# Three edits to a fused three-block network kernel: a weight tile split one stage earlier, residual rows scaled between convolved tiles, and the last norm done by token halves

## The chip, the cores and the metric

The kernel runs on one core of one Trainium2 chip. The metric is the time of one execution in device microseconds (us). TensorE is PE (its weight loads PEld), VectorE DVE, ScalarE ACT, GpSimd POOL; SyncE (SP) issues most DMAs.

## What is computed

Three different residual blocks run one after the other over 1024 tokens of width 1024, all in float32. Each block normalises, projects in, mixes, projects out, and adds a feed-forward part; then comes that block's own final norm. Cut to what the change touches:

```python
def second_block(x, w_in, ln1_g, ln2_g, lnf_g, ...):
    h = rmsnorm_2(x, ln1_g[l])
    p = h @ w_in[l]                       # 32 tiles of 128 columns
    ...                                   # qk = silu(causal conv of 4 taps), recurrences
    x = x + y @ w_out[l]
    h = rmsnorm_2(x, ln2_g[l])
    x = x + (jax.nn.silu(h @ w_gate[l]) * (h @ w_up[l])) @ w_down[l]
    return rmsnorm_2(x, lnf_g)

def third_block(x, ...):
    h = rms_norm(x, norm_mix[l])
    proj = jnp.einsum("bsd,dc->bsc", h, w_in[l])   # 25 tiles
    ...
    ff = jnp.square(jax.nn.relu(jnp.einsum("bsd,df->bsf", h, w_ff1[l])))
    x = x + jnp.einsum("bsf,fd->bsd", ff, w_ff2[l])
    return rms_norm(x, norm_final)
```

## The kernel before

**Layout and stages.** Activations lie transposed: the residual `g.h` is 8 tiles of 128 features (partitions) by 1024 tokens. The program is a row of stages; a stage ends when all five engines meet at a barrier. The stages that matter are the dense in-projections (`dense`, called as in1, in2, in3) and the second half of each block (`back`, as ff1, ff2, ff3: out-projection, middle norm, feed-forward part). `tidy` at the very end, and `sweep` inside a stage, clear the semaphores that the stage before used, half of them on POOL and half on SP.

**A product.** float32 products run as three fp32r matmuls, so every 128x1024 weight tile is split into a rounded part and a rest: `split_hi` (ACT, L186) and then `split_lo` (POOL, L192), into one of two weight buffers. `product` (L221 to L223) makes 48 matmuls of 128x512 for one output tile, 24 for each half of the tokens, into one of two groups of four PSUM banks. A tile needs three things: its split weights (`lo`), a free accumulator (`free`, given when DVE has read the tile before it in the same banks), and its right-hand side.

**From ff1 to in2, and from ff2 to in3.** `back` already starts the next dense stage: it loads four weight tiles of the next in-projection, splits two of them and makes their two products (tiles 0 and 1 of the dense stage) on the unnormalised residual; the norm's factor per token is applied when DVE empties the accumulator. Between and behind these products come the sums of squares (matmuls with a matrix of ones, L278) and the roots (`roots_of` on ACT: logarithm and exponential, each with a table load, L291 to L300; `scale_of` on DVE). The dense stage starts with `begun=True`: `grant` on POOL gives the starting counts of the semaphores (L166, L173), tile 2 is then split, and DVE empties tiles 0 and 1. The residual itself must still be multiplied by the norm's factor and gain: `scaled_rows` (L324), 8 instructions of 128x1024 on DVE, whose factor lies in `c.tot[0]`. When all 8 are done (`n_whole`), SP stores the residual (`spill`, at tile 7, L400).

**in2.** Tiles 0 to 3 are convolved (`convolved`): DVE reads the accumulator (L470), runs 4 taps (L479, L481, L482), ACT applies Silu (L418), stores the tile, and only then splits the next weights, since one ACT loop does both. The 8 `scaled_rows` stand behind the L470 of tile 0. From tile 4 on, one DVE instruction a tile is left (L502), and from tile 8 on a side job (`rwkv_beside`) runs beside the products.

**in3.** Tiles 0 to 8 are not convolved (L489), and 2 `scaled_rows` already stand behind each of tiles 0 to 3; a side job (`spatial_beside`, L4242 to L4312) starts at tile 0.

**ff3 and the end.** ff3 has no next stage. Its last tile (48 matmuls) is added to the residual over all tokens (L1243), squared on ACT (L337), added to the sum (L362), summed over the features on PE (L278), and turned into the root on ACT (L291, L294). The stage ends. `last_norm` is a stage of its own: DVE multiplies 6 rows of 128x1024 (L1298), ACT and POOL two (L1304, L1312), SP stores 8 rows of 512 KB (L1319), and the sweeps of ff3's semaphores run in it; `tidy` follows.

## Time and profile before

| | |
|---|---|
| median of 3 runs | 4217.23 us (4214.6 to 4221.69) |
| the profiled execution, its own time | 4217.12 us |
| its span (first to last instruction) | 4215.4 us |
| mean granted PE clock over the span | 0.94 |
| busy: PE, DVE, ACT, POOL | 88%, 65%, 38%, 26% |

A row of the timeline reads: start in us from the beginning of the span, length in us, engine, line, operation, output <- input with its size, and a count where equal ones in a row are merged; in square brackets the engine's idle time before it and what ended that. "SPq", "POOLq" are the engines' instruction queues. In the rows on one source line the durations are ns (least/median/greatest), then the first and last start in us.

### The profile page before, as it was taken

Reading aid. Unit: us, or ns where it says so; the run is one execution under the profiler, and the core shown is the slowest. Engines: PE = TensorE matmul, PEld = TensorE weight load, DVE = VectorE, ACT = ScalarE, POOL = GpSimd, SP = SyncE. Lnnn points to the kernel's source line nnn. Section 1 sums busy time; section 2 is a strip of 40 time slices with the busy share of each in tenths; the row PEclk is TensorE's granted clock in tenths of the full one; section 3 lists DMA queues with packets and bytes.
Section 4 is the critical chain, followed back from the end, with each engine's and each line's share of the span. In section 5 each row is a group of like instructions: output and inputs, shape, how many; then the busy total and the mean of one; then the engine's idle time right before and its main releaser. Section 6 shows DMA issues by size and latency. Waiting matters only on the chain. (4 is left out here: it accounts for less than half of the span.)

```text
span 4215.4 us, 46865 instructions
## 1 busy us (share of the span) xinstructions
PE 3710.3 (88%) x17658; PEld 3087.9 (73%) x17658; DVE 2728.3 (65%) x2977; ACT 1617.3 (38%) x2171; POOL 1113.3 (26%) x875
## 2 busy tenths in 40 slices
PE   9965999999989986856999999999933979999997
PEld 8953778788878776745788877878823957887886
DVE  3668688767544555366678877544859447887673
ACT  2503444433322234235433343354144564444332
POOL 1110222444212210200232244222120412224441
PEclk9987999999999998978999999999966989999998
DMA  4310255644143322242333344222272442556531
GB/s 137 104 51 15 66 160 160 211 154 134 46 140 109 112 83 58 76 152 78 106 101 111 105 156 144 80 85 85 90 185 52 137 149 75 170 160 196 163 120 60
DMA packets 525702, 482.38 MB, mean 114 GB/s; under 512 B 103237, under 2 KB 415045, under 8 KB 525481
## 3 DMA queue, kind: packets, MB, share of 16 engines
q1 hardware_dynamic: 516120, 445.22, 34.6%
q10 hardware_dynamic: 9360, 34.21, 2.0%
q8 instruction: 139, 2.28, 0.2%
q14 instruction: 83, 0.67, 0.1%
HBM read 321.77 MB, written 157.60 MB: 114 GB/s over the span
## 5 line engine op out<-in xcount | busy, mean ns | idle before, releaser
L921 POOL TENSOR_TENSOR c_wlo<-ff_spare,c_whi 128x512 fp32r<-128x512 f32 x200 | 322.0, 1611 | 573.9 <-ACT c_whi L755 573.6
L979 PE MATMUL c_acc<-c_hi,c_whi 128*128 128x512 f32 x928 | 362.4, 391 | 8.8 <-issue 8.8
L981 PE MATMUL c_acc<-c_lo,c_whi 128*128 128x512 f32 x928 | 361.6, 390 | 0.0
L982 PE MATMUL c_acc<-c_hi,c_wlo 128*128 128x512 f32 x928 | 361.5, 390 | 0.0
L192 POOL TENSOR_TENSOR w_wlo<-w_raw,w_whi 128x1024 fp32r<-128x1024 f32 x60 | 156.1, 2601 | 676.5 <-ACT w_whi L186 676.5
L755 ACT ACTIVATE c_whi<-ff_spare 128x512 fp32r<-128x512 f32 x315 | 198.0, 629 | 343.8 <-PE c_acc L982 329.9
L979 PE MATMUL c_acc<-ff_quad,c_whi 128*128 128x512 f32 x696 | 275.7, 396 | 18.4 <-DVE ff_quad L1219 5.5
L1150 DVE TENSOR_TENSOR h<-h,c_acc 128x512 f32<-128x512 f32 x265 | 176.8, 681 | 164.3 <-PE c_acc L982 164.2
L981 PE MATMUL c_acc<-ff_quad,c_whi 128*128 128x512 f32 x696 | 274.0, 394 | 0.0
L982 PE MATMUL c_acc<-ff_quad,c_wlo 128*128 128x512 f32 x696 | 274.0, 394 | 0.0
L192 POOL TENSOR_TENSOR c_wlo<-c_raw,c_whi 128x1024 fp32r<-128x1024 f32 (+1 forms) x53 | 129.4, 2441 | 451.9 <-ACT c_whi L186 451.9
L921 POOL TENSOR_TENSOR w_wlo<-ff_spare,w_whi 128x512 fp32r<-128x512 f32 x99 | 162.8, 1646 | 273.2 <-ACT w_whi L755 273.1
L221 PE MATMUL c_acc<-c_hi,w_whi 128*128 128x512 f32 x512 | 205.9, 402 | 12.3 <-POOL w_wlo L192 12.3
L979 PEld LDWEIGHTS c_acc<-c_hi,c_whi 128*128 128x128 f32 x928 | 174.7, 188 | 48.0 <-issue 11.2
L186 ACT ACTIVATE w_whi<-w_raw 128x1024 fp32r<-128x1024 f32 x60 | 63.5, 1059 | 361.3 <-PE c_acc L223 323.2
L982 PEld LDWEIGHTS c_acc<-c_hi,c_wlo 128*128 128x128 f32 x928 | 174.5, 188 | 36.5
L981 PEld LDWEIGHTS c_acc<-c_lo,c_whi 128*128 128x128 f32 x928 | 174.6, 188 | 35.9
L222 PE MATMUL c_acc<-c_lo,w_whi 128*128 128x512 f32 x512 | 200.6, 392 | 0.0
L223 PE MATMUL c_acc<-c_hi,w_wlo 128*128 128x512 f32 x512 | 200.4, 391 | 0.0
L221 PE MATMUL c_acc<-pair,w_whi 128*128 128x348 f32 (+1 forms) x512 | 177.1, 346 | 20.3 <-POOLq L166 20.3
L979 PE MATMUL c_acc<-c_hi,w_whi 128*128 128x512 f32 x448 | 174.6, 390 | 4.1 <-issue 4.1
L502 DVE TENSOR_TENSOR c_xs<-c_acc,c_xs 128x1024 f32<-128x1024 f32 x33 | 40.4, 1225 | 207.3 <-PE c_acc L223 198.1
(720 smaller groups left out, 10069.5 us busy)
## 6 DMA issues: line engine op xcount, KB each, us to landing
c_xs<-hidden SPq DMA_DIRECT2D x67, 1024.0 KB, 8.5
hidden<-c_xs SPq DMA_DIRECT2D x32, 1024.0 KB, 5.4
hidden<-h SPq DMA_DIRECT2D x62, 512.0 KB, 2.8
proj<-c_xs ACTq DMA_DIRECT2D x49, 512.0 KB, 2.6
w_raw<-in_w_in SPq DMA_DIRECT2D x48, 512.0 KB, 4.2
c_raw<-in_w_ff SPq DMA_DIRECT2D x36, 512.0 KB, 5.3
ff_spare<-in_w_ff SPq DMA_DIRECT2D x28, 512.0 KB, 6.7
h<-proj SPq DMA_DIRECT2D x25, 512.0 KB, 5.9
```

Source lines behind the costliest of these rows:

```text
L186: act.activation(s.whi[b][:, 0:kt, :], raw[:, 0:kt, :], ACT.Copy).then_inc(s.hi[b], 1)
L192: pool.tensor_tensor(s.wlo[b][:, 0:kt, :], raw[:, 0:kt, :], s.whi[b][:, 0:kt, :].bitcast(F32), ALU.subtract).then_inc(s.lo[b], 1)
L221: pe.matmul(out, s.whi[b][:, k, :], x_hi, start=(k == 0), stop=False)
L222: pe.matmul(out, s.whi[b][:, k, :], x_lo, start=False, stop=False)
L223: mm = pe.matmul(out, s.wlo[b][:, k, :], x_hi, start=False, stop=(k == kt - 1))
L502: dve.tensor_tensor(sliced(stg[b][:, 0:T], T), acc(b), sliced(g.inv[:, 0:T], T), ALU.mult)\
L755: act.activation(ring(s.whi, n), weight_of(n), ACT.Copy).then_inc(s["w_up"], 1)
L921: pool.tensor_tensor(ring(s.wlo, n), weight_of(n), ring(s.whi, n).bitcast(F32), ALU.subtract)\
L979: pe.matmul(to, hi[:, k, :], q_hi[q][:, k, :], start=fresh and k == 0, stop=False, skip_group_check=not fresh)
L981: pe.matmul(to, hi[:, k, :], q_lo[q][:, k, :], start=False, stop=False, skip_group_check=not fresh)
L982: mm = pe.matmul(to, lo[:, k, :], q_hi[q][:, k, :], start=False, stop=k == HK - 1, skip_group_check=not fresh)
L1150: tt(h, h, bank(p, name_), ALU.add).then_inc(s["ev"], 1)
```

## The change

1. ff1 and ff2 also split the third weight tile of the next in-projection (`split_hi` and `split_lo` for `total + 1`), ahead of the roots; the dense stage leaves the split of its tile 2 out, and `grant` gives one more count for it.
2. The norm's factor moves from `c.tot[0]` to `c.sq`. In a convolved start (in2) the 8 `scaled_rows` no longer stand behind the first L470: 2 follow behind the taps of each of tiles 0 to 3.
3. `last_norm` is gone. ff3 makes its last tile by halves of 512 tokens: 24 matmuls, then the ones-matmuls of the 7 rows so far, then the other 24. Each half is added, squared, summed, and rooted by itself, the root once into PSUM (for DVE) and once into SBUF (for POOL). DVE multiplies 12 half rows in place, POOL 4, and SP stores 16 pieces of 256 KB. ff3's 86 semaphores (75 before) are now cleared in `tidy`.

```diff
             pool.sem_inc(s.landed[b], 16)
+        pool.sem_inc(s.hi[0], 1)
+        pool.sem_inc(s.lo[0], 1)
...
-    to = c.inv[:, 0:SEQ] if how == "one" else c.tot[0][:, 0:SEQ]
+    to = c.inv[:, 0:SEQ] if how == "one" else c.sq
...
-        dve.scalar_tensor_tensor(h, h, g.par[:, gain + k:gain + k + 1], c.tot[0][:, 0:SEQ], ALU.mult, ALU.mult)\
+        dve.scalar_tensor_tensor(h, h, g.par[:, gain + k:gain + k + 1], c.sq, ALU.mult, ALU.mult)\
            .then_inc(s["n_whole"], 1)
...
-                    if it + 2 < tiles:
+                    if it + 2 < tiles and not (begun and it == 0):
                         split_hi(act, s, it % 2, it // 2 + 1, KD)
...
-                    split_lo(pool, s, it % 2, it // 2, KD)
+                    if not (begun and it == 2):
+                        split_lo(pool, s, it % 2, it // 2, KD)
...
-                    if it == 0 and head is not None:
-                        scaled_rows(dve, s, g, c, head_gain, off)
-                        dve.wait_ge(s["n_whole"], KD)
...
                        .then_inc(s[f"conv{b}"], 1)
+                    if it < 4 and head == "given":
+                        scaled_rows(dve, s, g, c, head_gain, off, (2 * it, 2 * it + 1))
...
+BY_POOL = (2, 5)
+LAST = ("f_made", "f_add", "f_sq", "f_sum", "f_log", "f_root", "f_copy", "f_gain", "f_dve", "f_pool", "f_out")
...
+                if ending is not None:
+                    for j in range(2):
+                        for n, k in enumerate(k for k in range(KD) if k not in BY_POOL):
+                            sp.wait_ge(s["f_dve"], (KD - len(BY_POOL)) * j + n + 1)
+                            sp.dma_start(ending[1][k * P:k * P + P, j * HALF_T:j * HALF_T + HALF_T], part(k, j))\
+                              .then_inc(s["f_out"], 16)
+                            if k - 1 in BY_POOL:
+                                n = BY_POOL.index(k - 1)
+                                sp.wait_ge(s["f_pool"], len(BY_POOL) * j + n + 1)
+                                sp.dma_start(ending[1][(k - 1) * P:k * P, j * HALF_T:j * HALF_T + HALF_T], part(k - 1, j))\
+                                  .then_inc(s["f_out"], 16)
+                    sp.wait_ge(s["f_out"], 16 * 2 * KD)
 
...
+                if ending is not None:
+                    gain = ending[0]
+                    for k in BY_POOL:
+                        act.activation(hk(k), hk(k), ACT.Copy, scale=g.par[:, gain + k:gain + k + 1]).then_inc(s["f_gain"], 1)
+                    act.wait_ge(s["n_eps"], 1)
+                    act.wait_ge(s["n_tot_a"], KD - 2)
+                    for j in range(2):
+                        act.wait_ge(s["f_add"], j + 1)
+                        act.activation(half(c.sq, j), part(KD - 1, j), ACT.Square).then_inc(s["f_sq"], 1)
+                        act.wait_ge(s["f_sum"], j + 1)
+                        act.activation(half(c.inv, j), s.psum[:, 2 + j, :], ACT.Ln, scale=1.0 / D, bias=c.low[:, 0:1])\
+                           .then_inc(s["f_log"], 1)
+                        act.wait_ge(s["f_log"], j + 1)
+                        act.activation(s.psum[:, 2 + j, :], half(c.inv, j), ACT.Exp, scale=-0.5).then_inc(s["f_root"], 1)
+                        act.activation(half(c.inv, j), half(c.inv, j), ACT.Exp, scale=-0.5).then_inc(s["f_copy"], 1)
                 if then is not None:
                     split_hi(act, s, 0, total, KD)
-                tail_scalar(act, s, g, end, KD - 1)
+                    tail_scalar(act, s, g, end, KD - 1)
                 if then is not None:
                     split_hi(act, s, 1, total, KD)
-                roots_of(act, s, c, how)
+                    split_hi(act, s, 0, total + 1, KD)
+                    roots_of(act, s, c, how)
...
+                    split_lo(pool, s, 0, total + 1, KD)
+                if ending is not None:
+                    for j in range(2):
+                        for n, k in enumerate(BY_POOL):
+                            pool.wait_ge(s["f_gain"], n + 1)
+                            pool.wait_ge(s["f_copy"], j + 1)
+                            pool.tensor_tensor(part(k, j), part(k, j), half(c.inv, j), ALU.mult).then_inc(s["f_pool"], 1)
...
+                def last_tile(it):
+                    def part_of(j, k):
+                        w_hi, w_lo, to = s.whi[1][:, k, :], s.wlo[1][:, k, :], s.psum[:, 4 + j, :]
+                        pe.matmul(to, w_hi, half(xhi[k], j), start=k == 0, stop=False)
+                        pe.matmul(to, w_hi, half(xlo[k], j), start=False, stop=False)
+                        return pe.matmul(to, w_lo, half(xhi[k], j), start=False, stop=k == last_k - 1)
+
+                    def squares(j):
+                        pe.wait_ge(s["f_sq"], j + 1)
+                        pe.matmul(s.psum[:, 2 + j, :], g.ones[:, :], half(c.sq, j), start=False, stop=True)\
+                          .then_inc(s["f_sum"], 1)
+
+                    pe.wait_ge(s.lo[1], it + 2)
+                    pe.wait_ge(s.free[1], it + 1)
+                    for k in range(last_k):
+                        mm = part_of(0, k)
+                    mm.then_inc(s["f_made"], 1)
+                    pe.wait_ge(s["n_tot_a"], KD - 2)
+                    for j in range(2):
+                        pe.matmul(s.psum[:, 2 + j, :], g.ones[:, :], half(c.tot[0], j), start=True, stop=False)
+                    for k in range(last_k):
+                        if k == last_k - 2:
+                            squares(0)
+                        mm = part_of(1, k)
+                    mm.then_inc(s["f_made"], 1)
+                    squares(1)
+
...
-                        product(pe, s, b, outs + j, xhi, xlo, T, last_k, each=rest if j == 0 and b == 0 else None)
+                        if ending is None or (j, b) != (KD // 2 - 1, 1):
+                            product(pe, s, b, outs + j, xhi, xlo, T, last_k, each=rest if j == 0 and b == 0 else None)
+                if ending is not None:
+                    last_tile(outs + KD // 2 - 1)
                 if then is not None:
                     product(pe, s, 0, total, *u, T, KD, halves_of="n")
                     pe.wait_ge(s["n_tot_b"], KD - 1)
-                pe.wait_ge(s["n_tot_a"], KD - 1)
-                sums_of(pe, s, g, c, how)
-                if then is not None:
+                    pe.wait_ge(s["n_tot_a"], KD - 1)
+                    sums_of(pe, s, g, c, how)
                     product(pe, s, 1, total, *u, T, KD)
...
+                        if ending is not None and k == KD - 1:
+                            return
...
-def last_norm(nc, g, c, gain, out):
...
+                if ending is not None:
+                    def added(j):
+                        dve.wait_ge(s["f_made"], j + 1)
+                        tt(part(KD - 1, j), part(KD - 1, j), s.psum[:, 4 + j, :], ALU.add).then_inc(s["f_add"], 1)
+
+                    def whole(j):
+                        gain = ending[0]
+                        dve.wait_ge(s["f_root"], j + 1)
+                        for k in range(KD):
+                            if k == KD - 1:
+                                dve.wait_ge(s["f_sq"], j + 1)
+                            if k not in BY_POOL:
+                                stt(part(k, j), part(k, j), g.par[:, gain + k:gain + k + 1], s.psum[:, 2 + j, :], ALU.mult,
+                                    ALU.mult).then_inc(s["f_dve"], 1)
+
+                    added(0)
+                    added(1)
+                    whole(0)
+                    whole(1)
 
 
...
-    back_half(nc, g, a, c, 3, 0, "w_out_3", "w_ff1_3", "w_ff2_3", 4 * KD, False, None, None, dram, early=early, restore=kept)
-    g.use(6, False)
-    last_norm(nc, g, c, g.col["gf3"], out)
+    back_half(nc, g, a, c, 3, 0, "w_out_3", "w_ff1_3", "w_ff2_3", 4 * KD, False, None, None, dram, early=early, restore=kept,
+              ending=(g.col["gf3"], out))
...
```

**Order of instructions, DVE, start of in2** (`c_acc` is the accumulator, `c_xs` holds the convolution's rows, `par` the taps and gains). Before:

```order
L387 MEMSET c_xs 128x1027
L470 TENSOR_TENSOR c_xs<-c_acc,c_xs 128x1024
L324 SCALAR_TENSOR_TENSOR h<-h,par,c_xs 128x1024 x8
L108 ISA
L479 TENSOR_SCALAR c_xs<-c_xs,par 128x1024
L481 SCALAR_TENSOR_TENSOR c_xs<-c_xs,par 128x1024 x2
L482 SCALAR_TENSOR_TENSOR c_xs<-c_xs,par 128x1024
L470 TENSOR_TENSOR c_xs<-c_acc,c_xs 128x1024
```

After the change:

```order
L389 MEMSET c_xs 128x1027
L473 TENSOR_TENSOR c_xs<-c_acc,c_xs 128x1024
L108 ISA
L479 TENSOR_SCALAR c_xs<-c_xs,par 128x1024
L481 SCALAR_TENSOR_TENSOR c_xs<-c_xs,par 128x1024 x2
L482 SCALAR_TENSOR_TENSOR c_xs<-c_xs,par 128x1024
L326 SCALAR_TENSOR_TENSOR h<-h,par,c_xs 128x1024 x2
L473 TENSOR_TENSOR c_xs<-c_acc,c_xs 128x1024
```

The 8 multiplications of `h` have left the place between the first read of the accumulator and the taps; two now stand behind the taps of tile 0, and two behind those of each of the next three.

**Order of instructions, ACT, end of ff1 and start of in2** (`w_whi` is the rounded half of a weight tile). Before:

```order
L186 ACTIVATE w_whi<-w_raw 128x1024
L291 ACT_TABLE_LOAD
L291 ACTIVATE c_xs<-c_acc,c_low 128x1024
L294 ACT_TABLE_LOAD
L294 ACTIVATE c_xs<-c_xs 128x1024
L298 ACT_TABLE_LOAD
L298 ACTIVATE c_xs<-c_xs,c_low 128x1024
L300 ACT_TABLE_LOAD
L300 ACTIVATE c_xs<-c_xs 128x1024
L631 UNCONDITIONAL_BRANCH
L412 UNCONDITIONAL_BRANCH
L186 ACTIVATE w_whi<-w_raw 128x1024
L418 ACT_TABLE_LOAD
L418 ACTIVATE c_xs<-c_xs 128x1024
L422 DMA proj<-c_xs 128x1024
L186 ACTIVATE w_whi<-w_raw 128x1024
```

After the change:

```order
L188 ACTIVATE w_whi<-w_raw 128x1024 x2
L293 ACT_TABLE_LOAD
L293 ACTIVATE c_xs<-c_acc,c_low 128x1024
L296 ACT_TABLE_LOAD
L296 ACTIVATE c_xs<-c_xs 128x1024
L300 ACT_TABLE_LOAD
L300 ACTIVATE c_xs<-c_xs,c_low 128x1024
L302 ACT_TABLE_LOAD
L302 ACTIVATE c_xs<-c_xs 128x1024
L637 UNCONDITIONAL_BRANCH
L414 UNCONDITIONAL_BRANCH
L420 ACT_TABLE_LOAD
L420 ACTIVATE c_xs<-c_xs 128x1024
L424 DMA proj<-c_xs 128x1024
L188 ACTIVATE w_whi<-w_raw 128x1024
```

One weight split has moved from behind the stage's end (the first instruction of in2) to ahead of the first table load of the roots.

**Order of instructions, ACT, end of ff3 and the last norm.** Before:

```order
L337 ACTIVATE c_xs<-h 128x1024 x3
L291 ACT_TABLE_LOAD
L291 ACTIVATE c_xs<-c_acc,c_low 128x1024
L294 ACT_TABLE_LOAD
L294 ACTIVATE c_xs<-c_xs 128x1024
L631 UNCONDITIONAL_BRANCH
L1301 UNCONDITIONAL_BRANCH
L1304 ACTIVATE flat<-h,par 128x1024 x2
```

After the change:

```order
L339 ACTIVATE c_xs<-h 128x1024 x2
L931 ACTIVATE h<-h,par 128x1024 x2
L936 ACTIVATE c_xs<-h 128x512
L938 ACT_TABLE_LOAD
L938 ACTIVATE c_xs<-c_acc,c_low 128x512
L941 ACT_TABLE_LOAD
L941 ACTIVATE c_acc<-c_xs 128x512
```

The same seven rows (from the square to the exponential into `c_xs`) follow once more for the second half; two multiplications by the gain stand ahead of the first square. There are four table loads where there were two.

**The same place, POOL** (L45 and L53 ISA are the clearing of semaphores). Before:

```order
L192 TENSOR_TENSOR c_wlo<-c_raw,c_whi 128x1024 x8
L631 UNCONDITIONAL_BRANCH
L1307 UNCONDITIONAL_BRANCH
L45 ISA x38
L1312 TENSOR_TENSOR flat<-flat,c_xs 128x1024 x2
L1294 UNCONDITIONAL_BRANCH
L50 UNCONDITIONAL_BRANCH
L53 ISA x2
```

After the change:

```order
L955 TENSOR_TENSOR c_wlo<-ff_spare,c_whi 128x512 x9
L194 TENSOR_TENSOR c_wlo<-c_raw,c_whi 128x1024 x8
L978 TENSOR_TENSOR h<-h,c_xs 128x512 x4
L637 UNCONDITIONAL_BRANCH
L50 UNCONDITIONAL_BRANCH
L53 ISA x43
L49 UNCONDITIONAL_BRANCH
```

The 38 clearings ahead of POOL's multiplications are gone, and 43 stand behind the last barrier but one, where 2 stood.

## Rows read from the trace of the kernel before

**Rows 1.** Page, busy time of each engine.
```profile
PE 3710.3 (88%) x17658; PEld 3087.9 (73%) x17658; DVE 2728.3 (65%) x2977; ACT 1617.3 (38%) x2171; POOL 1113.3 (26%) x875
```
**Rows 2.** Busy time by stretch, the start of in2; column before DMA: granted PE clock.
```profile
1175.00:1200.00 25.00, 12.83 (x49) 10.19 (x49) 23.96 (x18) 4.45 (x4) 5.28 (x2) 0.87 0.13 43
```
**Rows 3.** Timeline, PE, the start of in2.
```profile
1179.89 0.79 PE L221 MATMUL c_acc<-c_hi,w_whi 128*128 128x512 f32 x1 [4.99 <-POOL w_wlo L192]
...
1199.92 0.79 PE L221 MATMUL c_acc<-c_hi,w_whi 128*128 128x512 f32 x1 [7.28 <-POOL w_wlo L192]
```
**Rows 4.** Timeline, DVE, the start of in2.
```profile
1176.42 1.22 DVE L470 TENSOR_TENSOR c_xs<-c_acc,c_xs 128x1024 f32<-128x1024 f32 x1
1177.56 11.74 DVE L324 SCALAR_TENSOR_TENSOR h<-h,par,c_xs 128x1024 f32<-128x1024 f32 x8
...
1190.31 2.60 DVE L481 SCALAR_TENSOR_TENSOR c_xs<-c_xs,par 128x1024 f32<-128x1024 f32 x2
...
1196.39 4.57 DVE L481 SCALAR_TENSOR_TENSOR c_xs<-c_xs,par 128x1024 f32<-128x1024 f32 x2
...
1212.93 1.23 DVE L470 TENSOR_TENSOR c_xs<-c_acc,c_xs 128x1024 f32<-128x1024 f32 x1 [2.56 <-PE c_acc L223]
...
1223.81 1.23 DVE L502 TENSOR_TENSOR c_xs<-c_acc,c_xs 128x1024 f32<-128x1024 f32 x1 [2.77 <-PE c_acc L223]
```
**Rows 5.** Timeline, ACT, end of ff1 and start of in2.
```profile
1162.37 1.28 ACT L291 ACT_TABLE_LOAD   x1 [7.28 <-PE c_acc L278]
...
1194.27 1.06 ACT L418 ACTIVATE c_xs<-c_xs 128x1024 f32<-128x1024 f32 x1 [15.54 <-DVE c_xs L482]
...
1195.80 1.06 ACT L186 ACTIVATE w_whi<-w_raw 128x1024 fp32r<-128x1024 f32 x1 [0.47 <-ACT c_xs L418]
```
**Rows 6.** Timeline, POOL, the start of in2.
```profile
1196.93 2.94 POOL L192 TENSOR_TENSOR w_wlo<-w_raw,w_whi 128x1024 fp32r<-128x1024 f32 x1 [17.09 <-ACT w_whi L186]
```
**Rows 7.** Timeline, PE, after pauses of about 3 us (in ff2 and ff3).
```profile
2515.62 0.47 PE L979 MATMUL c_acc<-ff_quad,c_whi 128*128 128x512 f32 x1 [2.77 <-DVE h L1105]
...
3569.12 0.67 PE L979 MATMUL c_acc<-ff_quad,c_whi 128*128 128x512 f32 x1 [3.25 <-issue]
```
**Rows 8.** Loads of in2's third and fourth weight tiles in ff1 (L179), landing.
```profile
L179 SPq DMA_DIRECT2D w_raw<-in_w_in x2: 368/368/368, 1147.1 to 1158.0; - x2
...
DMA to landing us min/median/max: 4.0/4.1/4.1
```
**Rows 9.** Store of the whole residual (L400, twice in the program), landing.
```profile
DMA to landing us min/median/max: 12.8/15.4/18.1
```
**Rows 10.** Timeline, DVE and PE, the start of in3.
```profile
2773.61 1.23 DVE L489 TENSOR_TENSOR flat<-c_acc,c_xs 128x1024 f32<-128x1024 f32 x1
...
2778.12 3.78 PE L4242 MATMUL c_acc<-flat,ones 128*128 128x512 f32 x4 [6.03 <-ACT flat L4280]
```
**Rows 11.** Timeline, all engines, from ff3's last matmul to the end.
```profile
4186.94 0.39 PE L223 MATMUL c_acc<-ff_edge,c_wlo 128*128 128x512 f32 x1
...
4190.99 3.39 PE L278 MATMUL c_acc<-c_xs,ones 128*128 128x512 f32 x4 [3.66 <-DVE c_xs L362]
4194.46 1.28 ACT L291 ACT_TABLE_LOAD   x1 [4.78 <-PE c_acc L278]
...
4199.55 11.43 DVE L1298 SCALAR_TENSOR_TENSOR flat<-h,par,c_xs 128x1024 f32<-128x1024 f32 x6 [8.62 <-PEq L631]
4200.86 10.48 SPq L1319 DMA_DIRECT2D out_t<-flat  x8
```
**Rows 12.** Source lines: DVE reading PSUM by 128x512; clearings in a middle `tidy`.
```profile
L1150 DVE TENSOR_TENSOR h<-h,c_acc x265: 672/680/689, 830.6 to 4103.6; 128x512 f32<-128x512 f32 x133
...
L53 POOLq EVENT_SEMAPHORE_RANGE_CLEAR  x27: 44/44/44, 3060.7 to 3062.5; - x27
```
**Rows 13.** Busy time by stretch, the last stores; last columns: DMA share, GB/s.
```profile
4212.00:4213.00 1.00, 0.00 (x0) 0.00 (x0) 0.00 (x0) 0.00 (x0) 0.00 (x0) 0.50 1.00 393
```
**Rows 14.** Waits of ACT, rest of in2: us in total, times, longest.
```profile
ACT w_whi L186 <- DMA w_raw<-in_w_in: 28.6, 2, 14.3
```

39 lines of the change are left out of this document (7 added, 32 removed).

## The prediction

> **What bounds the kernel now.** I read the page first: PE is busy for 88% of the span, DVE for 65% [rows 1], so a gain has to come from stretches in which PE stands still. The waits of PE by line and its timeline show two in the start of in2: 4.99 us and 7.28 us, both ended by POOL's split of a weight tile [rows 3]. The table by stretch shows what it costs: from 1175 to 1200 us PE is busy for 12.83 of 25 us at a granted clock of 0.87, part of it at 1.2 GHz [rows 2]. Later in in2 no such pause is left: the accumulator reads follow each other by 10.88 us (1223.81 less 1212.93 [rows 4]), which is one product of 48 matmuls at 0.227 us. The program's end is a chain from PE over DVE, ACT and PE to ACT, then DVE's scaled rows and the stores [rows 11]. The time predicted is that of the profiled execution (4217.1 us, 0.1 us below the median of 4217.23), less what the steps save. A difference of 0.2% (8.4 us) is about what a measurement of this kernel can tell from no change.
>
> **Part 1, in2's start.** Why PE waits: tile 2's split begins only behind the barrier, and tile 3's split stands on ACT behind the Silu of tile 0 (1194.27, 15.54 us of idle ahead of it [rows 5]), which waits for tile 0's taps, which wait on DVE for the 8 scaled rows, 11.74 us [rows 4].
>
> Tile 2 after the change: its weights are there, so the last condition is the free accumulator, which DVE gives at 1176.42 + 1.22 = 1177.65 [rows 4]. PE starts there, 2.2 us earlier than at 1179.89 [rows 3].
>
> Tile 3: on DVE the taps of tile 0 now follow at once: 0.76 + 2.60 + 1.28 (with the two taps of [rows 4] as long as where POOL was still), so they end at about 1182.5. Silu, store and split follow on ACT as before: the split began 1.53 us after the Silu began [rows 5], so at 1184.2, and POOL, needing 2.94 us [rows 6], ends at about 1188.4. Tile 2 ends on PE at 1177.65 + 10.88 = 1188.5 or later, so tile 3 follows without a pause. The 7.28 us go, and so do its slow first matmuls: tile 3 ran from 1199.92 to about 1212.88, 2.1 us over 10.88. Tile 2 ran 12.75 us, 1.9 us over. Whether it still does is not settled: its pause is now 2.75 us (1177.65 less 1174.90, that is 1179.89 less 4.99). After a pause of 2.77 us the matmuls came at full speed (one of 0.47 us), after 3.25 us at half speed (0.67) [rows 7]. I take half of the 1.9 us back. Together 2.2 + 7.3 + 2.1 + 0.9 = **12.5 us** (11.6 if tile 2's slow matmuls stay, 13.5 if all go).
>
> Does DVE keep up with PE afterwards? Per convolved tile: 1.23 read, 0.76, 4.57 (two taps while POOL splits, 2.60 without [rows 4]), 1.28, and two scaled rows of 1.27: 10.4 us against 10.88. Started at 1185.1, DVE reads tile 2 at 1195.5 and tile 3 at 1205.9, both ahead of the products that need the banks (1200 and 1211). ACT's splits of tiles 4, 5 and 6 come 2.5 to 3 us ahead of need. The spill now waits for scaled rows behind tile 3, at about 1216.3, where it was at 1217; it lands at most 18.1 us later [rows 9], at 1235, and the tile-8 weights behind it in SP's queue are needed at 1241. From there in2 is bound by PE up to its end, so the 12.5 us stay.
>
> In ff1 and ff2 the added split costs nothing. Its tile is issued at 1147.1 and lands in 4.1 us [rows 8]; ACT is idle for 7.28 us up to 1162.37 [rows 5] and the split, 1.06 us, can run once the first product is done, two ones-matmuls of 0.9 us ahead of that, at about 1160.5. POOL's 2.4 us then end at 1164.1, while DVE is idle. If that cover were gone, each of two stages would pay up to 1.1 us on ACT. The two added counts in `grant` lie ahead of 1177.65.
>
> **Part 1, in3's start.** PE waits there not for weights but for a square on ACT, until 2778.12 [rows 10]. ACT's queue held the tile-2 split (1.06 us), a table load, the gelu and the square. Without the split the gelu waits for DVE's read, which ends at 2773.61 + 1.23 = 2774.84 [rows 10], and the two activations end at 2777.1. **1.0 us.** The table load, which waits for nothing, hides ahead of the read. The scaled rows of in3 do not move.
>
> **Part 2, the factor in another buffer,** costs nothing by itself: the same instructions read other columns.
>
> **Part 3, the end.** The last tile starts 47 x 0.2266 ahead of its last matmul at 4186.94 [rows 11], at 4176.3. First half: 24 matmuls, 5.4 us, 4181.7. DVE adds 512 tokens (0.68 [rows 12]), ACT squares by 4183.2, hidden behind PE: two ones-matmuls and 18 of the second half (about 0.9 each for the former at full speed, half of the 1.7 of [rows 11]), to 4187.6, the square's sum to 4188.4, the other 6 to 4189.8. ACT: table load 1.28, logarithm 0.6, table load 1.28, exponential 0.6: root in PSUM at 4192.4, second copy at 4193.0. Only then can ACT square the second half (4193.65), PE sums it after a pause of 3.8 us at half speed (1.7 us, as after 3.66 us in [rows 11]), 4195.4, and ACT repeats its four steps: 4199.4. DVE multiplies 6 half rows of 0.68 us, not slowed by POOL since a factor from PSUM held 672 to 689 ns over 265 instructions [rows 12]: the first half ends at 4196.5, the second at 4203.4, where before the six rows ended at 4211.0 [rows 11]. The stores bind then: 2.1 MB at 393 GB/s [rows 13] is 5.3 us, from about 1.7 us after the first piece at 4200.1, and 0.6 us to the end: 4207.8, where it was 4214.6. So 6.8 us saved. Against that, `tidy` clears 43 semaphores on POOL where it cleared 2; 27 took from 3060.7 to 3062.5 [rows 12], 0.069 us each, so 2.8 us more, with nothing beside it. Net **3.9 us** (bounds: 1.2 if the stores drain no faster than ready-made rows did, 6 if the ones-matmul runs at full speed and stores overlap better).
>
> Here a rule speaks against the change. In the rows the activation follows 1.29 us after the load's start (4194.46 [rows 11]). The Trainium skill, "ScalarE: Activation LUTs", "What ACT_TABLE_LOAD costs", counts about 2.66 us for every switch, a drain of 1.38 us included; four switches by that figure instead of the row's would add 5.5 us to the new chain and leave the end 1.6 us slower than before. I go by the row.
>
> **Sum.** 12.5 + 1.0 + 3.9 = 17.4; 4217.1 - 17.4 = **4199.7 us**. This case has a chance of 0.64, with 4196.5 to 4203.5 by its own bounds.
>
> **Rivals.**
>
> (a) *The two extra table loads cost double at the end*, each preceded by a drain as long as itself: 4 x 1.28 = 5.1 us on the halves' chain, 4204.8. For it: the loads now stand in front of a waiting PE. Against: 1.29 us in every row here. 0.13.
>
> (b) *DVE becomes the bound in in2's first tiles.* If POOL's split holds up one more DVE instruction by 2 us a tile, a tile takes 12.4 us, tiles 3 to 5 come late, and of the 12.5 us some 6 are lost: 4205.7. For it: the 10.4 us against 10.88 is thin. 0.12.
>
> (c) *in2's gain is lost before its end*, because the side job or a later stage waits for something that did not move, such as the spill: 4199.7 + 12.5 = 4212.2. Against: no pause of PE in in2 is ended by a DMA. 0.08.
>
> (d) *Slower: the third tile's weights land late in ff1 and ff2.* ACT's queue is strict, so the split waiting for its load holds back the roots, with them every engine and the barrier. In in2 ACT has waited twice for a weight load, 14.3 us at most, 28.6 in total [rows 14]. With such a wait in both stages: 4199.7 + 28.6 = 4228.3. It decides from a landing 9.4 us later than now (1160.6 against 1151.2), and makes the kernel slower by over 0.2% from 13 us of added wait in each stage. Against: 4.1 us in every such load in ff1 [rows 8]. 0.03.
>
> **How the numbers follow.** Faster by over 0.2% (below 4208.8): the forecast, (a) and (b), 0.89; within 0.2%: (c), 0.08; slower: (d), 0.03. The range 4195.5 to 4207 holds the forecast with both bounds, (a) and (b), leaving out (c), (d) and the edges.
>
> **What would show it.** Right: in in2 PE's tile 2 starts 2.2 us earlier against the barrier, has no pause ahead of tile 3, and DVE's second read comes 8.7 us after the first; in in3 the ones-matmul starts 1 us earlier against the barrier; at the end two groups of six half rows of 4 us with some 3 us between, a square on ACT just after the second exponential, and about 3 us from the last barrier but one to the end. Wrong: a pause of PE in tiles 4 to 6 of in2 ended by DVE (b) or by ACT in ff1 (d), table loads with 1.4 us of idle around them (a), or in2 as long as before (c).

## The result, and the profile after

The changed kernel took 4195.51 us (median of 6 runs, 4192.05 to 4198.39), the kernel before 4219.17 us (6 runs, 4214.6 to 4221.76; the three runs shown at the start are among them). The ratio is 0.9943, with an interval of 0.9933 to 0.9954: 24 us faster, between 19 and 28. The forecast was 17.4 us. The direction and the two terms of the in-projections hold; the term of the end came out at half its size, and a wait in it was wrong. In a second series the ratio was 0.9947 (0.9934 to 0.9960), 4197.03 against 4218.67 us. One execution each of e_load_held (6898.93 us) and h_best (14221.94 us) was disturbed and is left out of the medians below.

The profiled execution took 4195.38 us and its span 4193.6 us, against 4217.1 and 4215.4. First the page's busy times and the stretch table of in2's start, the same 25 us as [rows 2]:

```profile
PE 3710.5 (88%) x17662; PEld 3087.3 (74%) x17662; DVE 2719.0 (65%) x2983; ACT 1621.1 (39%) x2178; POOL 1108.4 (26%) x877
...
1175.00:1200.00 25.00, 22.11 (x98) 18.05 (x97) 23.38 (x19) 5.75 (x6) 4.79 (x2) 1.00 0.26 85
```

PE's sum has not moved (3710.3 in [rows 1]): the work is the same. In the stretch PE is busy for 22.1 us in place of 12.8, at the full clock (granted 1.00 in place of 0.87). The timeline of PE, the starts of in2 and in3, answers to [rows 3] and [rows 10]:

```profile
1179.78 0.47 PE L223 MATMUL c_acc<-c_hi,w_whi 128*128 128x512 f32 x1 [2.89 <-DVE c_xs L473]
...
2764.86 3.78 PE L4299 MATMUL c_acc<-flat,ones 128*128 128x512 f32 x4 [4.97 <-ACT flat L4337]
```

In in2 one pause is left, 2.89 us, and DVE's read ends it, no longer POOL's split. The 7.28 us ahead of tile 3 are gone. In in3 the wait for the square is 4.97 in place of 6.03 us. The timeline of DVE, in2's start, against [rows 4]:

```profile
1177.45 0.91 DVE L389 MEMSET c_xs<- 128x1027 f32 x1 [0.98 <-PEq L637]
1178.40 1.22 DVE L473 TENSOR_TENSOR c_xs<-c_acc,c_xs 128x1024 f32<-128x1024 f32 x1
1179.66 0.75 DVE L479 TENSOR_SCALAR c_xs<-c_xs,par 128x1024 f32<-128x1024 f32 x1
...
1184.29 2.48 DVE L326 SCALAR_TENSOR_TENSOR h<-h,par,c_xs 128x1024 f32<-128x1024 f32 x2
1186.68 1.22 DVE L473 TENSOR_TENSOR c_xs<-c_acc,c_xs 128x1024 f32<-128x1024 f32 x1
1187.94 2.10 DVE L479 TENSOR_SCALAR c_xs<-c_xs,par 128x1024 f32<-128x1024 f32 x1
```

The second read comes 8.3 us after the first (17.9 before). A tile then takes DVE 9.6 us, in which POOL's split holds up one instruction (2.10 in place of 0.75). PE needs 10.88, so DVE keeps ahead. ACT's timeline, against [rows 5]:

```profile
1184.41 1.06 ACT L420 ACTIVATE c_xs<-c_xs 128x1024 f32<-128x1024 f32 x1 [5.96 <-DVE c_xs L482]
...
1185.95 1.06 ACT L188 ACTIVATE w_whi<-w_raw 128x1024 fp32r<-128x1024 f32 x1 [0.47 <-ACT c_xs L420]
```

Tile 3's split stands at 1185.95, 7.6 us after the first read began, where it stood 19.4 us behind it (1195.80 less 1176.42). The end, rows of ACT, PE and DVE in the timeline and the closing clearings of POOL, against [rows 11]:

```profile
4168.53 0.63 ACT L936 ACTIVATE c_xs<-h 128x512 f32<-128x512 f32 x1 [1.85 <-DVE h L1363]
4169.18 1.28 ACT L938 ACT_TABLE_LOAD   x1
4174.43 0.69 ACT L938 ACTIVATE c_xs<-c_acc,c_low 128x512 f32<-128x512 f32 x1 [3.97 <-PE c_acc L1039]
4175.14 1.28 ACT L941 ACT_TABLE_LOAD   x1
...
4178.12 1.28 ACT L938 ACT_TABLE_LOAD   x1
4179.55 0.69 ACT L938 ACTIVATE c_xs<-c_acc,c_low 128x512 f32<-128x512 f32 x1
...
4178.16 1.35 PE L1039 MATMUL c_acc<-c_xs,ones 128*128 128x512 f32 x2 [2.37 <-ACT c_xs L936]
...
4177.07 4.04 DVE L1372 SCALAR_TENSOR_TENSOR h<-h,par,c_acc 128x512 f32<-128x512 f32 x6 [0.55 <-ACT c_acc L941]
4182.18 4.04 DVE L1372 SCALAR_TENSOR_TENSOR h<-h,par,c_acc 128x512 f32<-128x512 f32 x6 [1.08 <-ACT c_acc L941]
...
L53 POOLq EVENT_SEMAPHORE_RANGE_CLEAR  x43: 44/44/44, 4190.3 to 4193.3; - x43
```

The line that was not foreseen is the second: the table load starts at 4169.18, right behind the square, 5.2 us ahead of the logarithm that needs it. In [rows 11] it started when the sum was there, with 4.78 us of idle in front of it.

Three stretches hold all that moved, each measured inside one profiled execution, from the start of one instruction to the start of another. **in2**: from the last product of the factor on DVE ahead of it (L316, before L314) to the read of tile 10. **in3**: from the same product to the third read of an accumulator. **End**: from the add of row 6 in ff3 (the "k=6 add" of the expectations) to the end of the span. The marks of in2 and of the end in the timeline of DVE, first of the kernel before, then of the changed one:

```profile
1173.26 1.23 DVE L314 TENSOR_TENSOR c_xs<-c_xs 128x1024 f32<-128x1024 f32 x1 [3.59 <-ACT c_xs L300]
...
1289.14 1.23 DVE L502 TENSOR_TENSOR c_xs<-c_acc,c_xs 128x1024 f32<-128x1024 f32 x1 [9.06 <-issue]
...
4176.49 1.22 DVE L1243 TENSOR_TENSOR h<-h,c_acc 128x1024 f32<-128x1024 f32 x1 [6.20 <-PE c_acc L223]
```
```profile
1175.25 1.22 DVE L316 TENSOR_TENSOR c_xs<-c_xs 128x1024 f32<-128x1024 f32 x1 [3.59 <-ACT c_xs L302]
...
1278.04 1.22 DVE L504 TENSOR_TENSOR c_xs<-c_acc,c_xs 128x1024 f32<-128x1024 f32 x1 [9.06 <-issue]
...
4162.29 1.22 DVE L1315 TENSOR_TENSOR h<-h,c_acc 128x1024 f32<-128x1024 f32 x1 [6.20 <-PE c_acc L225]
```

From the read of tile 10 to that of in2's last tile both kernels take 256.6 us (1545.76 less 1289.14, and 1534.66 less 1278.04). The rest is the span less the three stretches. The table gives all four for the fourteen profiles, in us; the two changed-kernel rows are the first and the last.

| kernel | in2 | in3 | end | rest |
|---|---|---|---|---|
| changed | 102.8 | 21.7 | 31.3 | 4037.8 |
| before | 115.9 | 23.6 | 38.9 | 4037.0 |
| a_rows | 107.7 | 22.2 | 39.0 | 4038.1 |
| b_split | 114.3 | 21.7 | 39.5 | 4040.9 |
| c_end | 117.0 | 22.3 | 31.4 | 4039.3 |
| e_load_held | 104.4 | 21.7 | 34.3 | 4039.0 |
| p_factor_sbuf | 104.4 | 21.7 | 34.5 | 4033.9 |
| q_square_first | 102.8 | 21.7 | 31.3 | 4037.9 |
| f_tidy_five | 102.8 | 21.7 | 30.4 | 4036.9 |
| s_swap_waits | 103.4 | 22.4 | 31.3 | 4039.8 |
| m_pads | 102.8 | 21.6 | 31.3 | 4036.5 |
| g_clear_early | 102.8 | 21.7 | 28.7 | 4038.0 |
| h_best | 102.7 | 21.2 | 28.7 | 4040.6 |
| i_after_again | 104.4 | 21.2 | 31.4 | 4037.4 |

### The profile page after: what moved, and what is told of

Read it like the earlier page. It is cut to its first block and busy times, and to the rows that moved or that the text cites. A ratio compares the mean times of both kernels' runs of the same rounds, so it can differ in the third digit from the quotient of the medians.

```text
span 4193.6 us, 46898 instructions
## 1 busy us (share of the span) xinstructions
PE 3710.5 (88%) x17662; PEld 3087.3 (74%) x17662; DVE 2719.0 (65%) x2983; ACT 1621.1 (39%) x2178; POOL 1108.4 (26%) x877
## 5 line engine op out<-in xcount | busy, mean ns | idle before, releaser
L225 PE MATMUL c_acc<-c_hi,w_wlo 128*128 128x512 f32 x512 | 199.3, 389 | 0.0
L1023 PE MATMUL c_acc<-c_hi,w_wlo 128*128 128x512 f32 x448 | 174.3, 389 | 0.0
```

Of the source, the lines that this page charges most:

```text
L225: mm = pe.matmul(out, s.wlo[b][:, k, :], x_hi, start=False, stop=(k == kt - 1))
L1023: mm = pe.matmul(to, lo[:, k, :], q_hi[q][:, k, :], start=False, stop=k == HK - 1, skip_group_check=not fresh)
```

## The experiments

Six kernels were run once each (p_factor_sbuf, q_square_first, f_tidy_five, s_swap_waits, m_pads, g_clear_early): their times say nothing of a few us, and only the stretches are compared.

**One part at a time.** a_rows is the kernel before with the scaled rows moved, and the factor in `c.sq` (not shown in the cut):

```diff
-                    if it == 0 and head is not None:
-                        scaled_rows(dve, s, g, c, head_gain, off)
-                        dve.wait_ge(s["n_whole"], KD)
...
+                    if it < 4 and head == "given":
+                        scaled_rows(dve, s, g, c, head_gain, off, (2 * it, 2 * it + 1))
```

> The kernel before with one part of the change: in in2 the scaled rows go two at a time behind the taps of tiles 0 to 3 (the factor kept in the other buffer); the weight splits and the end stay as before. My theory: this part alone takes away the pause of PE ahead of tile 3, since tile 3's split stood behind the Silu that stood behind the 8 rows. Measured from in2's own memset (1175.47 before) to the read of the first plain tile (1234.69 before) the stretch is 59.2 us before and 46.1 with the whole change; here I expect 49.5 to 50.5 (the 7.3 us pause and some 2 us of half-speed matmuls of tile 3 gone, tile 2 still starting at 4.4 us, not at 2.3, after the memset). Time: 9 to 10 us less than before. Rival 1, the splits are what matters and the rows only pay with them: under 3 us. Rival 2, all of in2's gain is the rows': 13 us. The end's stretch and in3's start as before (38.9 us from the k=6 add to the end).

Measured: ratio 0.9973 (0.9962 to 0.9984), 4207.12 against 4218.92 us. From in2's memset to the read of tile 5 (the second plain one, which the expectation calls the first) it is 51.0 us, outside the 49.5 to 50.5 expected; over the stretch of the table 8.8 us less than the mean of the two profiles with the old in2 (116.4). PE in its timeline and the stretch table:

```profile
1179.43 0.79 PE L221 MATMUL c_acc<-c_hi,w_whi 128*128 128x512 f32 x1 [4.99 <-POOL w_wlo L192]
...
1175.00:1200.00 25.00, 20.57 (x79) 16.73 (x80) 24.60 (x18) 6.59 (x6) 7.13 (x3) 0.86 0.26 87
```

The first pause is as before, the second has gone. What was missed is the speed of tile 2: from its first matmul to its last 13.5 us pass here, 12.4 in the profile before. So the rows did stand in front of tile 3's split, and moving them is by far the larger part. b_split is the kernel before with the splits alone (the cut leaves out the counts in `grant` and the split that the dense stage skips):

```diff
                     split_hi(act, s, 1, total, KD)
+                    split_hi(act, s, 0, total + 1, KD)
...
+                    if not (begun and it == 2):
+                        split_lo(pool, s, it % 2, it // 2, KD)
```

> The kernel before with only the third weight tile split in ff1 and ff2. My theory: in in2 the pause ahead of tile 2 shrinks by 2.2 us, but tile 3 still waits for its split behind the Silu, so the gain is swallowed ahead of tile 3: in2's stretch from memset to the first plain tile's read stays 58.5 to 59.5 us (59.2 before). In in3 the ones-matmul comes 1 us earlier and its matmuls are quicker: 1.9 us less from in3's memset to its third read (21.4 before, 19.5 with the whole change). Time: 2 to 3 us less than before. Rival 1: in2 gains its 2 us here too (4 to 5 us in all). Rival 2: the added split on ACT and POOL delays the ends of ff1 or ff2 by about 1 us each: time as before.

Measured: ratio 0.9997 (0.9987 to 1.0008), too coarse for a few us. The trace tells more, PE and DVE in in2:

```profile
1178.62 0.47 PE L223 MATMUL c_acc<-c_hi,w_whi 128*128 128x512 f32 x1 [2.89 <-DVE c_xs L473]
...
1198.66 0.80 PE L223 MATMUL c_acc<-c_hi,w_whi 128*128 128x512 f32 x1 [7.26 <-POOL w_wlo L194]
...
1178.39 9.64 DVE L326 SCALAR_TENSOR_TENSOR h<-h,par,c_xs 128x1024 f32<-128x1024 f32 x8
```

My theory failed here and its first rival held: in2 gains 2.1 us even with the old order of the rows (57.6 us on the expectation's scale). I had taken the Silu's place as fixed. But tile 2's split on POOL had run beside the 8 rows (11.74 us in [rows 4]), and without it they take 9.64, so the Silu and tile 3's split come 2.1 us earlier too. The split in ff1 and ff2 does not delay those stages. in3's pause is 4.97 us, as in the whole change. c_end is the kernel before with the new end alone, the third item of the change:

```diff
-    last_norm(nc, g, c, g.col["gf3"], out)
+              ending=(g.col["gf3"], out))
```

> The kernel before with only the new end. My theory: the end is independent of the rest and gives the 7.6 us that the trace of the whole change shows: from the k=6 add to the end of the span 31.3 us in place of 38.9; in2 and in3 as before (59.2 and 21.4 us). Time: 7 to 8.5 us less than before. Together with a_rows and b_split the parts then miss some 4 us of the whole change's gain, which would be an interaction in in2. Rival 1: the end's gain is the predicted 3.9 us and the rest drift between executions. Rival 2: part of the end's gain needs the rest (clock): 5 us.

Measured: ratio 0.9980 (0.9972 to 0.9989), 8.0 us, and 31.4 us for the end. The end is worth 7.8 us by itself, and neither rival stands. The three parts alone make 11.8 + 0.9 + 8.0 = 20.7 us by their medians. In in2, a_rows and b_split together give 8.8 + 2.1 = 10.9 us of the 12.9, so some 2 us come only with both. With both, tile 2 starts 2.1 us earlier than in a_rows, and PE, after a pause of 2.89 us instead of 4.99, makes it in 10.7 or 12.4 us from first matmul to last, instead of 13.5: the mean of the seven profiles with the new in2 is 2.0 us less.

**Why the end gained twice the forecast.** e_load_held is the whole change with one wait more, always met, ahead of the wait for the sum:

```diff
+                        act.wait_ge(s["n_eps"], 1)
                         act.wait_ge(s["f_sum"], j + 1)
                         act.activation(half(c.inv, j), s.psum[:, 2 + j, :], ACT.Ln, scale=1.0 / D, bias=c.low[:, 0:1])\
```

> The whole change, and in the end's loop one more wait (always met) ahead of the logarithm, so that the table load in front of the logarithm takes the wait for the sum, as it does in the kernel before. My theory of the end: the prediction was too dear by 2.6 us because it let both table loads wait for the sums, while in the changed kernel they run ahead. Then here both loads start only at the sums' end and the end grows by 2.6 us: 33.9 us from the k=6 add to the end (31.3), the second half's logarithm 5.1+2.6 us after the first's... in all the time is 2.6 us over the changed kernel's, 4198.1. Rival, the shortfall came from the quick ones-matmuls and the stores alone: the end stays 31.3 us. A third: the longer pause of PE ahead of the second squares-matmul (2.4 + 1.3 = 3.7 us) puts it at half speed, 0.35 us more: 34.2.

Measured: 34.3 us for the end (34.26), median 4201.05 us, ratio 0.9956 (0.9942 to 0.9970). ACT and PE in the timeline:

```profile
4177.23 1.28 ACT L939 ACT_TABLE_LOAD   x1 [5.32 <-PE c_acc L1040]
4178.52 0.69 ACT L939 ACTIVATE c_xs<-c_acc,c_low 128x512 f32<-128x512 f32 x1
...
4184.20 1.28 ACT L939 ACT_TABLE_LOAD   x1 [2.00 <-PE c_acc L1040]
...
4182.25 1.87 PE L1040 MATMUL c_acc<-c_xs,ones 128*128 128x512 f32 x2 [3.70 <-ACT c_xs L936]
```

The third case of the expectation holds, and the rival, stores and ones-matmuls alone, does not. Of two waits directly ahead of the logarithm, the second is served in front of the table load, and the load starts when it is met; a single one stays behind the load, which runs as soon as ACT is free. No view shows which wait a load carries: this is read from the start times, here and in s_swap_waits below. The kernel before has two waits there (n_eps and the sum), the change waits for n_eps earlier, and so hides two loads. With the loads held PE also pauses for 3.70 us instead of 2.37, and its two matmuls take 1.87 us instead of 1.35. Counted from the add of row 6, DVE's two groups of rows start 1.3 and 3.2 us later than in the changed kernel; behind its last row 0.25 us comes back (7.13 us to the end of the span instead of 7.38), and the end grew by 2.95.

The kernel before shows the same in ff1, in the second logarithm of `roots_of`, which has one wait ahead of it. ACT in its timeline:

```profile
1167.18 1.28 ACT L298 ACT_TABLE_LOAD   x1
1169.71 1.15 ACT L298 ACTIVATE c_xs<-c_xs,c_low 128x1024 f32<-128x1024 f32 x1 [1.25 <-DVE c_xs L311]
```

The load starts 2.5 us ahead of its activation, which waits for DVE, while that of L291 with its two waits starts only at the sum's end ([rows 5]).

p_factor_sbuf tests another term, the price of the half rows:

```diff
-                        dve.wait_ge(s["f_root"], j + 1)
+                        dve.wait_ge(s["f_copy"], j + 1)
...
-                                stt(part(k, j), part(k, j), g.par[:, gain + k:gain + k + 1], s.psum[:, 2 + j, :], ALU.mult,
+                                stt(part(k, j), part(k, j), g.par[:, gain + k:gain + k + 1], half(c.inv, j), ALU.mult,
```

> The whole change, but at the end DVE takes the factor of its half rows from the copy in SBUF, as POOL does, not from PSUM. The prediction costed the half rows at 0.68 us each because the factor comes from PSUM and POOL then does not slow DVE; in the changed kernel six took 4.04 us. My theory: with all three operands in SBUF the rows that run while POOL multiplies take longer: six rows 6 to 8 us in place of 4.04 (in the kernel before, six full rows with the factor from SBUF took 11.43 us beside POOL, 1.9 each), and they start 0.6 us later, so that the end's stretch from the k=6 add to the end of the span is 34 to 36 us in place of 31.3. Rival, the half rows are quick whatever they read: six rows 4.0 us, only the 0.6 us of the later copy: 31.9 us.

Measured: 34.5 us, and DVE's rows without a gap between them, in the timeline and by source line:

```profile
4175.33 12.06 DVE L1372 SCALAR_TENSOR_TENSOR h<-h,par,c_xs 128x512 f32<-128x512 f32 x12 [1.10 <-ACT c_xs L942]
```
```profile
L1372 DVE SCALAR_TENSOR_TENSOR h<-h,par,c_xs x12: 736/740/1754, 4175.3 to 4186.7; 128x512 f32<-128x512 f32 x12
```

The twelve rows take 12.06 us in place of 8.08, 1.0 each on average. Most are as quick as before (median 740 ns, 742 in the changed kernel); some take up to 1754 ns, where the longest was 748, and POOL has four multiplications there. So reading the factor from PSUM is worth 3.2 us here, 0.6 of it the later start. A kernel that makes only the root in SBUF would have it one activation of 0.6 us earlier; that was not tried.

**What is left to take at the end.** q_square_first moves the second half's square ahead of the SBUF copy:

```diff
...
                         act.activation(s.psum[:, 2 + j, :], half(c.inv, j), ACT.Exp, scale=-0.5).then_inc(s["f_root"], 1)
+                        if j == 0:
+                            square(1)
```

> The whole change, but ACT squares the second half before it makes the SBUF copy of the first half's root. My theory: the second half's chain (square, sum, logarithm, exponential) binds the end, since its rows start only when its root is there: it starts 0.54 to 0.6 us earlier, and the pause of PE ahead of it is 1.8 us in place of 2.4: the end's stretch 30.7 us in place of 31.3. Rival, the stores bind: they move 380 to 400 GB/s from 1.7 us after the first issue to 4.2 us before the end, so the end stays at 31.3. Second rival: POOL's rows of the first half, 0.6 us later, run into the second half's: 31.3 or more.

Measured: 31.3 us, no gain, and for neither reason given. ACT in the timeline:

```profile
4177.05 0.61 ACT L936 ACTIVATE c_xs<-h 128x512 f32<-128x512 f32 x1
4177.56 0.61 ACT L947 ACTIVATE c_xs<-c_xs 128x512 f32<-128x512 f32 x1
4178.20 1.28 ACT L941 ACT_TABLE_LOAD   x1
4179.49 0.69 ACT L941 ACTIVATE c_xs<-c_acc,c_low 128x512 f32<-128x512 f32 x1
```

The square is earlier, but copy and table load now fill ACT until 4179.49. Its own queue binds, since both orders hold the same instructions ahead of the second logarithm. f_tidy_five spreads the closing clearing:

```diff
+        for n, add in enumerate((block.gpsimd, block.sync, block.vector, block.scalar, block.tensor)):
...
+                for sem in left_over.sems[n::5]:
+                    eng.sem_clear(sem)
```

> The whole change, but the closing clearing of semaphores (43 on POOL, 43 on SP, 3.0 us on POOL in the changed kernel) spread over all five engines, 17 or 18 on each. My theory: nothing lies beside the clearing, so the stretch after the last barrier but one shrinks from 3.0 to about 1.3 us: from the k=6 add to the end 29.6 us in place of 31.3. Rival: the time is the barrier's and not the clearing's, or DVE's, ACT's and PE's clearings are slower: 31.3.

Measured: 30.4 us, half of what I expected. The trace by source line:

```profile
L54 POOLq EVENT_SEMAPHORE_RANGE_CLEAR  x18: 44/44/44, 4189.4 to 4190.6; - x18
L54 SPq EVENT_SEMAPHORE_RANGE_CLEAR  x17: 25/25/25, 4189.5 to 4190.3; - x17
...
L54 PEldq EVENT_SEMAPHORE_RANGE_CLEAR  x17: 56/56/56, 4189.5 to 4191.5; - x17
```

PE's queue needs 2.0 us for 17 of them, 0.12 each, where POOL needs 0.07 and SP 0.05. g_clear_early puts 75 of the 86 clearings on ACT, behind its last activation in the program, once SP, POOL and DVE have passed the waits on them:

```diff
...
+                    act.wait_ge(s["f_dve"], 1)
+                    act.wait_ge(s["f_pool"], 1)
+                    act.wait_ge(s["f_sp"], 1)
+                    s.swept = [n for n in s if n not in LAST]
+                    for n in s.swept:
+                        act.sem_clear(s[n])
```

> The whole change, but ACT clears the 75 semaphores that nobody uses any more while DVE's last rows and the stores run (ACT is idle from 4182.7 of 4193.6), so that the closing clearing has 6 on POOL and 6 on SP in place of 43 and 43. My theory: the closing clearing is time with nothing beside it, 0.069 us each on POOL: 37 x 0.069 = 2.6 us less: from the k=6 add to the end 28.7 us in place of 31.3, time 2.6 us less than the changed kernel's. Spreading it over five engines gave 0.9 (30.4), since PE takes 0.12 us for each. Rival: 75 clearings on ACT, 4.5 us, end after the stores: 31.3 or more.

Measured: 28.7 us, as expected. The closing clearing on POOL, and the early one on ACT, by source line:

```profile
L53 POOLq EVENT_SEMAPHORE_RANGE_CLEAR  x6: 44/44/44, 4190.5 to 4190.9; - x6
...
L949 ACTq EVENT_SEMAPHORE_RANGE_CLEAR  x75: 41/41/46, 4180.6 to 4185.5; - x75
```

**The same rule elsewhere, and in2's start.** s_swap_waits changes the order of the two waits in `roots_of`:

```diff
-    act.wait_ge(s["n_eps"], 1)
     act.wait_ge(s[f"{of}_summed"], 1)
+    act.wait_ge(s["n_eps"], 1)
```

> The whole change, and in roots_of the two waits ahead of the logarithm in the other order, so that the table load in front of it takes the wait that is long met and the logarithm the wait for the sum (two places: ff1 and ff2). My theory, the same that explains the end: the load now starts as soon as ACT is through with the split, 0.64 us before the sum is ready, so the logarithm comes 0.64 us earlier against the end of the ones-matmuls in each stage (now 1.29 us after the load's start at the sum's end; then about 0.65). From the sum's end to the last root 10.9 us now, 10.2 then. Time 1.3 us less than the changed kernel's, not measurable in the median. Rival, a load is held up by whatever follows it: no difference.

Measured: ACT did as expected, the end of ff1 did not. The timeline, ACT and then DVE:

```profile
1163.64 1.28 ACT L293 ACT_TABLE_LOAD   x1
1164.93 1.11 ACT L293 ACTIVATE c_xs<-c_acc,c_low 128x1024 f32<-128x1024 f32 x1
...
1177.36 0.91 DVE L389 MEMSET c_xs<- 128x1027 f32 x1 [1.60 <-PEq L637]
```

The last root is 0.64 us earlier and the idle time ahead of in2's memset longer by the same: 1.60 us in place of 0.98 (its in2 and in3 in the table are longer by this, since they are counted from that root). The barrier between the stages waits for PE, whose product of tile 1 ends at 1176.80 (its last matmul starts at 1176.41 and takes 0.39). What hid on ACT there was worth nothing. m_pads shortens the memset:

```diff
-                dve.memset(xs, 0.0).then_inc(s["own"], 1)
+                if taps - 1 > lead:
+                    dve.memset(xs[:, lead + T:], 0.0)
+                dve.memset(xs[:, 0:lead], 0.0).then_inc(s["own"], 1)
```

> The whole change, and at the start of in2 and in3 DVE blanks only the 3 (in3: 4) columns beside the convolution's row, not all 1027. The memset, 0.91 us, stands on DVE between the barrier and the first accumulator read, on which PE's tile 2 waits. My theory: both starts come 0.85 us earlier against the last root's product (DVE L316: now 1175.25, first read 1178.40, PE's tile 2 1179.78): PE's pause ahead of tile 2 is 2.05 us in place of 2.89, in in3 4.1 in place of 4.97. From the barrier on everything of in2 and in3 follows. 1.7 us less in all. Whether tile 2's matmuls then come at full speed is not settled: with 2.89 us of pause they ran at half speed in some executions and not in others; after 2.05 us I expect full speed, up to 1.6 us more. Rival: DVE's first read waits for something else behind the barrier: 0.

Measured: PE's pause 2.83 us in place of 2.89; in2 and in3 are 0.1 us shorter at most, where 0.85 us each was expected. DVE in the timeline:

```profile
1175.76 0.06 DVE L391 MEMSET c_xs<- 128x3 f32 x1 [0.76 <-PEq L639]
1176.86 1.23 DVE L475 TENSOR_TENSOR c_xs<-c_acc,c_xs 128x1024 f32<-128x1024 f32 x1 [1.04 <-POOLq L172]
```

The rival held: the read waits for POOL, which gives the stage's first counts one by one in `grant` (L172), and they had been hidden behind the memset. Giving the counts in another order was not tried. Both edits together, and the changed kernel again beside them:

> Both together, the pads alone blanked and the clearing done early, on top of the whole change. By my theories 1.7 + 2.6 us less than the changed kernel: 4191.2 us against its 4195.5, and the end's stretch 28.7 us. Rival, in2's start gains more because its matmuls come at full speed: up to 4189.5. Rival, neither lies on the path: 4195.5.

> The changed kernel once more, beside h_best on the same chip, for the spread of what did not change: I expect 4195 to 4200 us, the end's stretch 31.3 us, in3's memset to third read 19.5 us, and in2's memset to last plain read either 100.6 us (tile 2 at full speed) or 102.2 (half speed for its first matmuls). The unchanged stretches between in2 and in3 may differ by 5 us from one execution to the next, as they do among the four kernels of the first call (1482.4 to 1487.4 us).

Measured: h_best 28.7 us at the end, ratio 0.9935 (0.9922 to 0.9948). Its end is 2.6 us shorter than that of i_after_again, its median 5.0 us lower (4192.02 against 4197.03). It is the best version found; what it has over the change in these stretches is the early clearing, since m_pads gave 0.1 us. The intervals of the two ratios overlap, so the 2.6 us rest on the traces.

## Why the prediction was right or wrong

**In2's start, 12.5 us: right.** 12.9 us is what the traces give, the mean of 115.9 and 117.0 less the mean of the seven with the new in2 unedited (103.5). The steps: tile 2 starts 4.5 us after the last product of the factor began where it started 6.6 us after it (2.1 us, forecast 2.2); the pause of 7.28 is gone; the second read 8.3 us after the first (forecast 8.7). The step I left half open, whether tile 2's matmuls still come slowly, has no single answer: four of the seven profiles lie at 102.8 us or so, three at 104.4. The 0.9 us I put for it is a mean of two outcomes, of which an execution has one, so the nearness of 12.5 to 12.9 is in part luck. The gain stayed up to the end of in2, as said.

**In3's start, 1.0 us: right,** though the two traces first seem to say 1.9. The wait shrinks by 1.06 us. The other 0.8 or so is the first profile's: its in3 took 23.6 us, while a_rows and c_end, whose in3 is also the old one, took 22.2. The means are 22.7 and 21.6.

**The end, 3.9 us: wrong,** 7.8 us. The failed step is "ACT: table load 1.28, logarithm 0.6, table load 1.28", taken to begin at the sum's end, in both halves: a wait in front of the first load that the runs do not show. The first load runs while ACT waits for the sum. That makes 2 x 1.28 us; and the pause ahead of the second sum is 2.37 us, not the 3.8 I gave, and the two matmuls behind it take 1.35 instead of 1.7 us. Together 2.9 us; with the loads held again, e_load_held is 2.95 us longer. I could have known: for in3 I let the load "which waits for nothing" hide, and the profile before has one that starts 2.5 us ahead of its activation (L298, above). The remaining 1.0 us lies in short things: from the end of DVE's last row to the end of the span 7.4 us where the working gave 8.0, roots that follow each other 0.1 us closer, the profiled old end, 38.9 us, 0.2 under the mean of the three (39.1), and a slip of 0.1 in my own sum (6.8 less 2.8 is 4.0). One sign listed as right did not come: between the two groups of half rows DVE rests 1.1 us, not some 3. The other terms hold: first product done at its place within 0.2 us, six half rows 4.04 us (4.1), closing clearing 3.0 us (2.8 more than before).

**The sum.** 12.9 + 1.05 + 7.8 = 21.75 us, against 17.4. The spans of the changed kernel's first profile and of that before differ by 21.8 us; that they agree so well is chance, since the untouched rest differs by 0.8 between the two; the medians by 23.7 and, in the second series, 21.6. The rest of the program, untouched by the change, took from 4033.9 to 4040.9 us in the fourteen profiles, so single executions differ by more than any of the small terms, and only stretches inside an execution can carry them. The forecast time of 4199.7 was 4.2 us too high; the measured one is at the low end of the range, 4195.5. The base was low too: the six executions of the kernel before have a median of 4219.17 us, 1.9 over the 4217.23 of the three I had, so the measured gain of 23.7 us is more than the 21.7 that my range allowed. The upper bound of 6 us that I gave the end was itself too tight.

**The rivals.** (a) Table loads at double price: refuted. Where nothing else holds the activation, it starts 1.28 to 1.30 us after its load's start (1.29 and 1.30 at L941, 1.29 in all four of e_load_held), and the other two of the four loads cost nothing. The figure of about 2.66 us for a switch in the Trainium skill, "ScalarE: Activation LUTs", "What ACT_TABLE_LOAD costs", is not what these rows show. (b) DVE as the bound in in2's first tiles: refuted, 9.6 us a tile against PE's 10.88. (c) in2's gain lost: refuted by the in2 column and the equal 256.6 us behind it. (d) Late weights in ff1 or ff2: did not occur; in ff1 the load landed in 4.1 us and ACT's wait there was ended by PE, 5.58 us. Each had its sign in the profile as listed, and none was there.

## What to carry to other kernels

Before costing an inserted load or any other helper instruction at its place in the source, see which wait it takes with it: two waits ahead of an activation held the table load, one let it run 5 us early. Whether that pays depends on who ends the stretch: 2.9 us at the program's end, where ACT binds, and nothing in ff1 and ff2, where a product on PE ends the stage. Look in the trace of before for a load of the same kind. And measure small terms inside an execution, from one landmark to the next, with several kernels that share the stretch; the difference of two spans had put 0.8 us of chance into in3.

## What the runs showed that I had not expected

- The granted clock after one and the same pause is not the same in each execution. After 2.89 us of pause ahead of tile 2 with the same product of tile 1 ahead of it, PE's next matmuls ran at the full 2.4 GHz in some executions (changed, q, f, s and g; also m and h after 2.83 us) and partly at 1.2 GHz (0.43 us from one to the next, not 0.227) in others (b, e, p and the repeat i). With the rows and the splits both moved, in2 takes 102.8 or 104.4 us by it, and nothing between; s_swap_waits has 102.8 and the 0.64 us of its earlier root. The old pause of 4.99 us was followed by 12.4 us for tile 2 in the profile before and 13.5 in a_rows and c_end. The stretch tables of the two kinds, the changed kernel and e_load_held, eleven us from tile 2's start on:

```profile
1179.70:1190.70 11.00, 10.93 (x48) 1.00 0.30 99
```
```profile
1177.50:1188.50 11.00, 10.93 (x41) 8.94 (x42) 10.82 (x9) 2.13 (x2) 2.40 (x1) 0.84 0.30 99
```

- POOL's split beside eight rows of DVE with both operands and the factor in SBUF costs DVE 2.1 us (11.74 against 9.64), so a split moved away pays on DVE as well as where it stood.
- Clearing a semaphore costs 0.07 us on POOL, 0.05 on SP and 0.12 on PE. ACT cleared 75 in 4.9 us while its own last activations, by the profile, still ran.
